# Reordering the key, query and value projections around the start of windowed attention in a two-layer decoder trunk

## The chip, the cores and the metric

The kernel runs on one core of a Trainium2 chip. The metric is device time in microseconds (us), the median over runs. The engines are TensorE (PE), VectorE (DVE), ScalarE (ACT), GpSimd (POOL) and SyncE (SP, which here issues the weight loads).

## The reference, cut to what matters

One sequence of 256 tokens of width 1024 passes through two layers. Layer 0 is a gated linear recurrence and a dense SwiGLU. Layer 1 is sliding-window attention (16 query heads, 4 key/value heads, head size 64, window 128) and a top-2-of-8 routed SwiGLU. The change touches the attention's front end alone:

```
hn = rmsnorm(h, kv_norm); k, v = split(hn @ kv_w, 2)      # 256 columns each
k = rmsnorm(k per head) ; q = rmsnorm((rmsnorm(h, attn_norm) @ w_q) per head)
logits = q @ k.T * scale + bias            # banded, window 128, 4 query heads a group
m = max(logits, sink); p = exp(logits - m)
out = (p / (sum(p) + exp(sink - m))) @ v ;  h = h + out @ w_o
```

The routed experts that follow take two thirds of the time and aren't changed.

## The kernel before

Every engine has its own program, written out by hand; they meet at semaphores. An engine runs its instructions in the order of its program, so one that waits holds up all that stands behind it.

**Dense weights.** All weights ahead of the experts form one stream of 1 MB chunks (`stream`), numbered `c`. SP loads chunk c into `raw`; ACT rounds it (`round_to`, L526, writes `w_hi`); DVE subtracts the rounded part (`rest_to`, L784, writes `w_lo`); PE multiplies in three products of the high and low parts (`product`, L1253 to L1255). `w_hi` and `w_lo` have three slots, so ACT rounds chunk c only when PE has used chunk c-3. A chunk costs PE 24 matmuls of 512 columns or 48 of 256. `to_rows` makes rows of tokens: `t` is one of two tiles of 128 tokens.

**Projections before.** Two chunks give keys and values together (256 rows of both widths are accumulated into `banks[0]` and `banks[1]`, each holding keys and values of a token tile). Then four chunks give the queries: each holds 256 rows of `w_q` at the full width of 1024, so that all 16 heads are complete only at the end of the fourth. They fill banks 2 to 5.

**The inputs of the projections.** They are the residual transposed and scaled by either gain, rounded by ACT (`fresh_round`, L553) and subtracted by DVE (`fresh_rest`, L798), first `kv_hi`/`kv_lo`, then `ht_hi`/`ht_lo`, each in four groups (token tile, half of the width).

**Normalisation.** Keys: ACT evicts `kk` and `ksq` (and the values `vt`), DVE sums the squares, ACT takes the root (`head_roots`, L538), DVE scales and writes `k2` twice. PE turns `k2` (L1472) ahead of the last query chunk and DVE copies it into `kT` (L1071). Queries: after the last chunk ACT squares (L700), DVE sums (L1078), ACT takes the roots, DVE scales into `xs` (L1086), PE turns them (L1485), DVE copies into `aqT` (`turn_copy`, L823).

**Attention.** For each of four groups g of heads, `logits(g)` on PE fills three banks: a bias product (L1458) and the logits (L1502). DVE takes maxima (`largest`, L1095 to L1102), ACT exponentials (L721 to L727), DVE normalises (`normalise`, L1107 to L1112), PE turns the probabilities in three banks (`turn_probs`, L1512), DVE copies them (`turn_copy` into `pTs`), PE multiplies by the values (`attend`, L1524 to L1526). On PE the order is logits(0), logits(1), then for each g turn_probs(g), logits(g+2), attend(g). Only two banks, `turn`, serve all transposes, in turn: a new one waits until the copy of the one before the last is done. The output projection follows in four chunks from `C_O`.

Of the kernel before, what the change touches and what calls it, by code (L numbers as in the profile page):

```python
# [8 lines left out]
P = 128  # L9
D = 1024  # L10
KT = D // P
# [9 lines left out]
FF = 2816  # L21
# [9 lines left out]
N_IN, N_OUT, N_FF, N_DOWN, N_KV, N_Q, N_O = 16, 4, 2 * FF // 256, FF // 256, 2, 4, 4  # L31
# [4 lines left out]
C_Q = C_KV + N_KV  # L36
C_O = C_Q + N_Q
# [40 lines left out]
def build_program(nc, a, out):  # L78
# [19 lines left out]
    stream += [flat(a["kv_w"], 512 * i, 512) for i in range(N_KV)]  # L98
    stream += [flat(a["swa_w_q"][0], 256 * i, 256) for i in range(N_Q)]
# [20 lines left out]
    with ctx:  # L120
# [390 lines left out]
        def _(act):  # L511
# [161 lines left out]
            round_to(C_KV + 1)  # L673
# [19 lines left out]
            round_to(C_O - 1 + LEAD)  # L693
            for t in range(TT):
                if t == 0:
                    act.wait_ge(tile_done, 1)
                else:
                    act.wait_ge(chunk_used, C_O)
                for half in range(2):
                    nc.scalar.activation(xs[:, t, 512 * half:512 * half + 512], banks[2 + 2 * t + half][:, :],  # L700
                                         ACT.Square, scale=tok_rstd[:, 2, t:t + 1]).then_inc(sq_ready, 1)
            for t in range(TT):
                head_roots(QH * t, QH, AD, 4 + 1 + t + 1)
# [9 lines left out]
            for g in range(KVH):  # L713
# [5 lines left out]
                l = banks[3 * (g % 2):3 * (g % 2) + 3]  # L719
# [7 lines left out]
                nc.scalar.activation(sinkd[:, g, :, :], sinkd[:, g, :, :], ACT.Exp).then_inc(exps_ready, 1)  # L727
            att_round(KVH - 2)
# [42 lines left out]
        def _(dve):  # L771
# [277 lines left out]
            rest_to(C_KV + 1)  # L1049
            for group in GROUPS:  # L1050
                fresh_rest(ht_hi, ht_lo, 8, LO_Q, group)
            rest_to(C_Q - 1 + LEAD)
            dve.wait_ge(kv_out, 3 * TT)
# [11 lines left out]
            rest_to(C_O - 2 + LEAD)  # L1065
# [9 lines left out]
            rest_to(C_O - 1 + LEAD)  # L1075
            for t in range(TT):
                dve.wait_ge(sq_ready, 4 + 2 * t + 2)
                nc.vector.tensor_reduce(ssq[:, QH * t:QH * t + QH], heads(xs[:, t, :]), AX.X, ADD).then_inc(ssq_ready, 1)  # L1078
            for t in range(TT):
                dve.wait_ge(root_ready, 4 + t)  # L1080
                part = rstd[:, QH * t:QH * t + QH]
                then(nc.vector.reciprocal(part, part))
                then(nc.vector.tensor_scalar(part, part, tok_rstd[:, 2, t:t + 1], None, MUL))
                for half in range(2):
                    n0 = QH * t + 8 * half
                    nc.vector.tensor_tensor(heads(xs[:, t, 512 * half:512 * half + 512]), heads(banks[2 + 2 * t + half][:, :]),  # L1086
                                            rstd[:, n0:n0 + 8].unsqueeze(2).to_broadcast([P, 8, AD]), MUL).then_inc(q_normed, 1)
            for t in range(TT):
                for u in range(2):
                    turn_copy(aqT[:, 4 * u:4 * u + 4, P * t:P * t + P])  # L1090

            def largest(g):
                l = banks[3 * (g % 2):3 * (g % 2) + 3]
# [27 lines left out]
            largest(0)  # L1121
            normalise(0)
# [14 lines left out]
            for t in range(TT):  # L1137
                for half in range(2):
                    add_part(C_MOE - 1, 6, (t, half), [banks[1], banks[2], banks[4], banks[5]][2 * t + half], None)
# [107 lines left out]
        def _(pe):  # L1247
# [69 lines left out]
            def to_rows(c, width, kts, k0, n_k, hi, lo, dst, since=None, tell=False, fresh=None, then_turn=None):  # L1317
# [4 lines left out]
                for t in range(TT):  # L1322
                    for q in range(max(1, width // 512)):
                        w = min(width, 512)
                        for k in range(kts):
# [3 lines left out]
                            if fresh is not None and q == k == 0:  # L1329
                                pe.wait_ge(fresh_lo, fresh[t])  # L1330
# [124 lines left out]
            def biases(g, b):  # L1455

                t, first, last = logit_banks[b]
                nc.tensor.matmul(banks[3 * (g % 2) + b][:, :], const[:, K_ANTI:K_ANTI + P],  # L1458
# [3 lines left out]
            for i in range(N_KV):  # L1462
                to_rows(C_KV + i, 512, 4, 4 * i, KT, kv_hi, kv_lo, lambda t, q: banks[t][:, :],
                        fresh=[LO_KV + 2 * t + i + 1 for t in range(TT)])
            for i in range(N_Q):
                if i == N_Q - 1:

                    pe.wait_ge(keys_ready, 2)
                    for t in range(TT):
                        bank = turn_bank()  # L1470
                        for g in range(KVH):
                            ins = nc.tensor.transpose(bank[:, P * g:P * g + P], k2[:, t, g, :, :].rearrange("p i e -> p (i e)"), ident)  # L1472
                        ins.then_inc(turned, 1)
# [217 lines left out]
```

## Time and profile before

| what | value |
|---|---|
| time of three runs | 1413.07, 1415.06, 1415.53 us; median 1415.06 |
| span of the profiled execution | 1414.1 us |
| PE, DVE, ACT, POOL busy | 95%, 24%, 18%, 2% of the span |
| mean granted TensorE clock | 0.983 of full speed |
| memory traffic | 442.50 MB, mean 313 GB/s |

The span runs from the first to the last instruction of one profiled execution; the time of that execution outside the profiler isn't given by itself, and the median of the runs is 1.0 us above its span. A busy share is that of the whole span. A matmul's length in the timeline overlaps with the next one's, since matmuls are pipelined: the step from start to start is what counts. "Idle before" is the time that an engine stood still ahead of an instruction, with what released it.

### The profile page before, as it was taken

To read this page: it belongs to the slowest core of one execution; us is meant where nothing else is said; L and a number is where in the kernel's file an instruction comes from. 1 tells how busy PE (TensorE), PEld (TensorE's weight loads), DVE (VectorE), ACT (ScalarE), POOL (GpSimd) and SP (SyncE) were. 2 spreads that over 40 slices of the span, in tenths; PEclk is the share of its full clock that TensorE was granted. 3 is DMA by queue.
4 is the path that set the end of the run, shared out by engine and by line. 5 is a ranking of instruction groups with operands and counts; after the bars stand their busy time and mean duration, and the time that the engine had idled before them with its cause. 6 is when DMAs were issued, how large, how long until landed. Compare 5 with 4: busy or idle time off the path is not lost.

```text
span 1414.1 us, 32772 instructions
## 1 busy us (share of the span) xinstructions
PE 1349.5 (95%) x14759; PEld 798.3 (56%) x14759; DVE 344.5 (24%) x485; ACT 260.5 (18%) x396; POOL 21.2 (2%) x27
## 2 busy tenths in 40 slices
PE   6998999999979699999999999999999999999994
PEld 6997899988757434534533543443453453453352
DVE  5864555545765401000000000000000100000001
ACT  5463544444632100000000000000000000000000
POOL 0001000000000100000000000000000000000001
PEclk9999999999989899999999999999999999999997
DMA  9962465554701896999999999999999999999994
GB/s 320 350 230 74 138 198 182 180 195 162 246 22 60 339 365 229 360 406 322 408 420 383 390 418 398 378 416 408 367 413 419 366 412 419 360 409 420 380 383 170
DMA packets 123701, 442.50 MB, mean 313 GB/s; under 512 B 9060, under 2 KB 50356, under 8 KB 107188
## 3 DMA queue, kind: packets, MB, share of 16 engines
q1 hardware_dynamic: 117600, 424.75, 79.3%
q10 hardware_dynamic: 4820, 11.53, 2.3%
q0 software_dynamic: 1152, 4.19, 0.8%
q8 instruction: 119, 1.95, 0.6%
q14 instruction: 10, 0.08, 0.0%
HBM read 434.12 MB, written 12.08 MB: 316 GB/s over the span
## 4 chain that ended last, share of the span: by engine, by line
PE 92%; DVE 4%; ACT 2%; DMA 1%; issue 1%; ACTq 0%; POOL 0%; POOLq 0%; DVEq 0%
PE bank L1607 41%; PE bank L1622 21%; PE bank L1253 8%; PE bank L1255 8%; PE bank L1254 8%; PE bank L1652 1%; PE bank L1502 1%; PE bank L1665 1%; PE bank L1597 1%; PE bank L1391 1%; PE bank L1458 1%; DVE w_lo L784 0%; PE bank L1589 0%; DMA raw<-slot_rows,slot 0%; ACT w_hi L526 0%
## 5 line engine op out<-in xcount | busy, mean ns | idle before, releaser
L1607 PE MATMUL bank<-raw,xT 128*32 128x512 f32 (+1 forms) x4608 | 440.8, 539 | 3.7 <-issue 3.0
L1607 PEld LDWEIGHTS bank<-raw,xT 128*32 128x32 f32 x4608 | 151.7, 110 | 282.1 <-issue 282.1
L1622 PE MATMUL bank<-dn,hidT 128*32 128x256 f32 x5376 | 296.5, 379 | 0.0
L1622 PEld LDWEIGHTS bank<-dn,hidT 128*32 128x32 f32 x5376 | 172.3, 110 | 116.1 <-issue 4.4
L784 DVE TENSOR_TENSOR w_lo<-raw,w_hi 128x2048 fp32r<-128x2048 f32 x62 | 141.8, 2291 | 117.7 <-ACT w_hi L526 117.6
L1228 DVE TENSOR_TENSOR e_hid<-e_silu,bank 128x512 f32<-128x512 f32 (+1 forms) x48 | 26.9, 616 | 530.4 <-PE bank L1607 530.4
L1607 PE MATMUL bank<-up_more,xT 128*32 128x384 f32 (+1 forms) x1536 | 150.3, 539 | 0.0
L1253 PE MATMUL bank<-ht_hi,w_hi 128*128 128x256 f32 x480 | 137.2, 286 | 4.2 <-DVE w_lo L857 2.7
L1255 PE MATMUL bank<-ht_hi,w_lo 128*128 128x256 f32 x480 | 136.8, 285 | 0.0
L1254 PE MATMUL bank<-ht_lo,w_hi 128*128 128x256 f32 x480 | 135.7, 283 | 0.0
L526 ACT ACTIVATE w_hi<-raw 128x2048 fp32r<-128x2048 f32 x62 | 118.1, 1912 | 61.6 <-PE bank L1255 61.6
L1607 PEld LDWEIGHTS bank<-up_more,xT 128*32 128x32 f32 x1536 | 50.9, 110 | 93.4 <-issue 93.4
L1253 PEld LDWEIGHTS bank<-ht_hi,w_hi 128*128 128x128 f32 x480 | 91.3, 190 | 5.5 <-issue 5.5
L1254 PEld LDWEIGHTS bank<-ht_lo,w_hi 128*128 128x128 f32 x480 | 92.4, 192 | 0.0
L1255 PEld LDWEIGHTS bank<-ht_hi,w_lo 128*128 128x128 f32 x480 | 90.9, 189 | 0.0
L756 ACT ACTIVATE hidT<-bank 128x512 f32<-128x512 f32 (+1 forms) x32 | 17.4, 545 | 386.2 <-PE bank L1652 205.3
L1253 PE MATMUL bank<-w_hi,ht_hi 128*128 128x256 f32 (+1 forms) x224 | 75.5, 337 | 1.2 <-DVE w_lo L784 1.2
L1254 PE MATMUL bank<-w_lo,ht_hi 128*128 128x256 f32 (+1 forms) x224 | 74.5, 332 | 0.0
L1255 PE MATMUL bank<-w_hi,ht_lo 128*128 128x256 f32 (+1 forms) x224 | 74.3, 332 | 0.0
L751 ACT ACTIVATE e_silu<-bank 128x512 f32<-128x512 f32 (+1 forms) x48 | 22.7, 544 | 244.3 <-PE bank L1607 244.3
L760 ACT ACTIVATE yb<-bank 96x512 f32<-96x512 f32 x8 | 4.7, 594 | 235.2 <-PE bank L1622 235.2
L1253 PEld LDWEIGHTS bank<-w_hi,ht_hi 128*128 128x128 f32 x224 | 42.6, 190 | 6.5 <-DVE w_lo L784 1.7
(246 smaller groups left out, 828.5 us busy)
## 6 DMA issues: line engine op xcount, KB each, us to landing
dn<-in_moe_w_down SPq DMA_DIRECT2D x112, 1024.0 KB, 12.6
raw<-in_moe_w_gate SPq DMA_DIRECT2D x48, 1024.0 KB, 13.5
raw<-in_moe_w_up SPq DMA_DIRECT2D x48, 1024.0 KB, 12.6
raw<-in_moe_w_gate SPq DMA_DIRECT2D x48, 768.0 KB, 9.3
raw<-in_moe_w_up SPq DMA_DIRECT2D x48, 768.0 KB, 6.3
up_more<-in_moe_w_gate SPq DMA_DIRECT2D x16, 1024.0 KB, 21.8
up_more<-in_moe_w_up SPq DMA_DIRECT2D x16, 1024.0 KB, 12.4
raw<-in_hgrn_w_in SPq DMA_DIRECT2D x15, 1024.0 KB, 12.1
```

What stands on the lines that cost most here:

```text
L526: nc.scalar.activation(w_hi[:, slot, :], raw[:, slot_raw, :], ACT.Copy).then_inc(hi_ready, 1)
L751: nc.scalar.activation(e_silu[:, j, 0:w], banks[j][:, 0:w], ACT.Silu).then_inc(e_silu_ready, 1)
L756: nc.scalar.activation(hidT[sup][:, :, j, :], src[:, 0:w].rearrange("p (k t) -> p k t", t=P), ACT.Copy).then_inc(hidT_ready, 1)
L784: nc.vector.tensor_tensor(w_lo[:, slot, :], raw[:, slot_raw, :], plain(w_hi[:, slot, :]), SUB).then_inc(split_ready, 1)
L1228: nc.vector.tensor_tensor(e_hid[:, j, 0:w], e_silu[:, j, 0:w], banks[GRPS + j][:, 0:w], MUL).then_inc(e_hid_ready, 1)
L1253: nc.tensor.matmul(dst, st[0], mv[0], start=first, stop=False)
L1254: nc.tensor.matmul(dst, st[0], mv[1], start=False, stop=False)
L1255: return nc.tensor.matmul(dst, st[1], mv[0], start=False, stop=last)
L1391: whole = lambda bank_rows, at, w, st, mv: nc.tensor.matmul(bank[bank_rows:bank_rows + CH, at:at + w], st, mv, start=True, stop=True)
L1458: nc.tensor.matmul(banks[3 * (g % 2) + b][:, :], const[:, K_ANTI:K_ANTI + P], bias_rev[:, GRP * g + first:GRP * g + last, 2 * P - P * (t + ...
L1607: ins = nc.tensor.matmul(out_banks[j][GTOK * c:GTOK * c + GTOK, 0:w], xT[:, kt, GTOK * g:GTOK * g + GTOK], chunk[:, w * b:w * b + w], star ...
L1622: ins = nc.tensor.matmul(banks[6 + j // 2][GTOK * c:GTOK * c + GTOK, 256 * (j % 2):256 * (j % 2) + 256], tok, dn[:, i % DN_RING, D * half ...
```

## The change

- The stream becomes: keys (one chunk, all 1024 rows of 256 columns), queries in four chunks of 512 rows and 512 columns (two for heads 0 to 7, two for heads 8 to 15), values (one chunk), then the output projection as before. The number of chunks and of bytes stays.
- PE: keys; query chunks 0, 1, 2; turn the keys; turn the first half of the queries; query chunk 3; `logits(0)`; turn the second half; the values; `logits(1)`; then the loop over g as before.
- ACT: key evictions ahead of the rounding of query chunk 2; squares and roots of each half of the queries apart (`query_roots`); values evicted after the exponentials of group 0.
- DVE: sums and scaling of the first half stand after the subtraction of query chunk 3, then the copies of the keys and of this half, then the subtractions of the value chunk and of the first output chunk, then the second half; the copies of the second half and the next subtraction stand between `largest(0)` and `normalise(0)`.
- Banks: keys in 0, values in 1, the query halves in 2, 3 and 4, 5; the logits in 2, 3, 0 and 4, 5, 1; the output in 2, 3, 0, 4.
- Query chunk 0 waits for two of the four groups of `ht_lo`, instead of all; the waits for `kv_lo` are by group too.

```diff
-    stream += [flat(a["kv_w"], 512 * i, 512) for i in range(N_KV)]
-    stream += [flat(a["swa_w_q"][0], 256 * i, 256) for i in range(N_Q)]
+    stream += [deep(a["kv_w"], 0, 256)]
+    for half in range(2):
+        stream += [flat(a["swa_w_q"][0][:, 512 * half:512 * half + 512], 512 * i, 512) for i in range(2)]
+    stream += [deep(a["kv_w"], 256, 256)]
...
+        LOGIT_BANKS = ([banks[2], banks[3], banks[0]], [banks[4], banks[5], banks[1]])
+        OUT_BANKS = [[banks[2], banks[3]], [banks[0], banks[4]]]
...
-            round_to(C_Q - 1 + LEAD)
-            act.wait_ge(chunk_used, C_Q)
+            round_to(C_Q + 1)
+            act.wait_ge(chunk_used, C_KV + 1)
             act.wait_ge(rstd_ready, 3)
             for t in range(TT):
                 mine = tok_rstd[:, 2, t:t + 1]
-                nc.scalar.activation(vt[:, t, :], banks[t][:, 256:512], ACT.Copy, scale=mine).then_inc(kv_out, 1)
-                nc.scalar.activation(kk[:, t, :], banks[t][:, 0:256], ACT.Copy, scale=mine).then_inc(kv_out, 1)
-                nc.scalar.activation(ksq[:, t, :], banks[t][:, 0:256], ACT.Square, scale=mine).then_inc(kv_out, 1)
+                keys = banks[0][:, 256 * t:256 * t + 256]
+                nc.scalar.activation(kk[:, t, :], keys, ACT.Copy, scale=mine).then_inc(kv_out, 1)
+                nc.scalar.activation(ksq[:, t, :], keys, ACT.Square, scale=mine).then_inc(kv_out, 1)
+            round_to(C_Q + 2)
             head_roots(0, TT * KVH, AD, 4 + 1)
             ta[0] += TT
...
+            def query_roots(half):
+
+                for t in range(TT):
+                    if t == 0:
+                        act.wait_ge(tile_done, half + 1)
+                    else:
+                        act.wait_ge(chunk_used, C_Q + 2 * half + 2)
+                    nc.scalar.activation(xs[:, t, 512 * half:512 * half + 512], banks[2 + 2 * half + t][:, :],
                                          ACT.Square, scale=tok_rstd[:, 2, t:t + 1]).then_inc(sq_ready, 1)
+                head_roots(QH * half, QH, AD, 4 + 1 + TT * (half + 1))
+
+            round_to(C_Q + 3)
+            query_roots(0)
+            round_to(C_O)
+            query_roots(1)
+            round_to(C_O + 1)
...
+                if g == 0:
+
+                    act.wait_ge(chunk_used, C_V + 1)
+                    for t in range(TT):
+                        nc.scalar.activation(vt[:, t, :], banks[1][:, 256 * t:256 * t + 256], ACT.Copy,
+                                             scale=tok_rstd[:, 2, t:t + 1]).then_inc(kv_out, 1)
...
-            rest_to(C_O - 2 + LEAD)
+            rest_to(C_Q + 3)
+
+            def query_sums(half):
+
+                for t in range(TT):
+                    dve.wait_ge(sq_ready, 4 + TT * half + t + 1)
+                    at = QH * half + 8 * t
+                    nc.vector.tensor_reduce(ssq[:, at:at + 8], heads(xs[:, t, 512 * half:512 * half + 512]), AX.X, ADD).then_inc(ssq_ready, 1)
+
+            def query_norms(half):
+
+                dve.wait_ge(root_ready, 4 + half)
+                both = rstd[:, QH * half:QH * half + QH]
+                then(nc.vector.reciprocal(both, both))
+                for t in range(TT):
+                    at = QH * half + 8 * t
+                    part = rstd[:, at:at + 8]
+                    then(nc.vector.tensor_scalar(part, part, tok_rstd[:, 2, t:t + 1], None, MUL))
+                    nc.vector.tensor_tensor(heads(xs[:, t, 512 * half:512 * half + 512]), heads(banks[2 + 2 * half + t][:, :]),
+                                            part.unsqueeze(2).to_broadcast([P, 8, AD]), MUL).then_inc(q_normed, 1)
+
+            query_sums(0)
+            query_norms(0)
             dve.wait_ge(keys_zeroed, 1)
             for t in range(TT):
                 dve.wait_ge(turned, td[0] + 1)
...
+                turn_copy(aqT[:, 0:4, P * t:P * t + P])
+            rest_to(C_O)
+            query_sums(1)
+            query_norms(1)
...
             largest(0)
+            for t in range(TT):
+                turn_copy(aqT[:, 4:8, P * t:P * t + P])
+            rest_to(C_O + 1)
             normalise(0)
             largest(1)
...
+            to_rows(C_KV, 256, KT, 0, KT, kv_hi, kv_lo, two_tiles(banks[0]),
+                    fresh={(t, 4 * half): LO_KV + 2 * t + half + 1 for t, half in GROUPS})
+            for i in range(N_Q - 1):
+                queries(i)
+            pe.wait_ge(keys_ready, 2)
+            for t in range(TT):
+                bank = turn_bank()
+                for g in range(KVH):
+                    ins = nc.tensor.transpose(bank[:, P * g:P * g + P], k2[:, t, g, :, :].rearrange("p i e -> p (i e)"), ident)
+                ins.then_inc(turned, 1)
+            turn_queries(0)
+            queries(N_Q - 1)
...
+            pe.wait_ge(bias_loaded, 16)
             logits(0)
+            turn_queries(1)
+            to_rows(C_V, 256, KT, 0, KT, kv_hi, kv_lo, two_tiles(banks[1]))
             logits(1)
```

`queries(i)` is `to_rows` of chunk `C_Q + i` into bank 2 + 2 half + t; `turn_queries(half)` is, for each token tile, a wait for `q_normed`, a bank of `turn` and four transposes.

## Rows read from the trace of the kernel before

**Rows 1.** The page: shares of the chain that ended last, by engine.
```profile
PE 92%; DVE 4%; ACT 2%; DMA 1%; issue 1%; ACTq 0%; POOL 0%; POOLq 0%; DVEq 0%
```

**Rows 2.** Windows: length; PE, PEld, DVE, ACT, POOL busy (count); clock; DMA share; GB/s.
```profile
387.00:412.10 25.10, 17.50 (x74) 12.48 (x73) 16.01 (x32) 7.98 (x31) 0.00 (x0) 0.81 0.13 43
412.10:436.00 23.90, 21.46 (x143) 15.36 (x141) 16.25 (x33) 9.76 (x46) 0.00 (x0) 0.92 0.00 1
...
489.30:1395.00 905.70, 901.83 (x11752) 398.69 (x11752) 52.54 (x96) 50.28 (x103) 0.00 (x0) 1.00 0.98 382
```

**Rows 3.** Timeline of PE: start us, length us, line, operation, idle before.
```profile
363.63 0.50 PE L1253 MATMUL bank<-w_hi,ht_hi 128*128 128x512 f32 x1 [1.24 <-DVE w_lo L784]
...
380.60 1.04 PE L1472 MATMUL bank<-const,pr 128*128 128x128 f32 x8
381.39 0.48 PE L1253 MATMUL bank<-w_hi,ht_hi 128*128 128x512 f32 x1
...
391.01 1.25 PE L1485 MATMUL bank<-const,xs 128*128 128x128 f32 x8 [2.05 <-DVE xs L1086]
394.05 1.94 PE L1485 MATMUL bank<-const,xs 128*128 128x128 f32 x8 [1.78 <-DVE aqT L823]
...
411.21 1.11 PE L1512 MATMUL bank<-const,pr 128*128 128x128 f32 x4 [2.41 <-DVE pT L823]
412.12 1.91 PE L1458 MATMUL bank<-bias_rev,const 128*128 128x512 f32 x2
...
419.34 0.43 PE L1524 MATMUL bank<-pT,vt 128*64 128x128 f32 x2
...
423.64 1.02 PE L1458 MATMUL bank<-bias_rev,const 128*128 128x512 f32 x2
...
428.93 0.43 PE L1524 MATMUL bank<-pT,vt 128*64 128x128 f32 x2
```

**Rows 4.** Timeline of PE in an earlier 256-column projection.
```profile
80.20 0.28 PE L1253 MATMUL bank<-w_hi,ht_hi 128*128 128x256 f32 x1
...
80.55 0.28 PE L1253 MATMUL bank<-w_hi,ht_hi 128*128 128x256 f32 x1
```

**Rows 5.** Timeline of DVE over the projections and the attention.
```profile
356.52 4.22 DVE L798 SCALAR_TENSOR_TENSOR ht_lo<-bank,cols,ht_hi 128x128 fp32r<-128x128 f32 x16
361.29 4.49 DVE L784 TENSOR_TENSOR w_lo<-raw,w_hi 128x2048 fp32r<-128x2048 f32 x2 [0.55 <-ACT w_hi L526]
...
369.06 2.28 DVE L784 TENSOR_TENSOR w_lo<-raw,w_hi 128x2048 fp32r<-128x2048 f32 x1
...
381.30 2.81 DVE L1071 COPY kT<-bank 64x512 f32<-64x512 f32 x4 [1.83 <-PE bank L1472]
...
390.27 1.29 DVE L1086 TENSOR_TENSOR xs<-bank,rstd 128x512 f32<-128x512 f32 x2
...
405.77 0.17 DVE L1107 TENSOR_TENSOR rsum<-rsum,sinkd 128x8 f32<-128x8 f32 x1 [3.50 <-ACT sinkd L727]
...
410.48 1.28 DVE L823 COPY pT<-bank 128x512 f32<-128x512 f32 x2
```

**Rows 6.** Timeline of ACT over the key and value evictions.
```profile
359.20 3.85 ACT L526 ACTIVATE w_hi<-raw 128x2048 fp32r<-128x2048 f32 x2
362.81 0.60 ACT L688 ACTIVATE vt<-bank,tok_rstd 128x256 f32<-128x256 f32 x1
...
364.59 0.65 ACT L690 ACTIVATE pr<-bank,tok_rstd 128x256 f32<-128x256 f32 x1
365.26 1.28 ACT L538 ACT_TABLE_LOAD   x1
366.56 0.30 ACT L538 ACTIVATE rstd<-ssq,eps 128x8 f32<-128x8 f32 x1
```

**Rows 7.** Windows of PE alone: length, busy (count), granted clock, DMA share, GB/s.
```profile
392.00:399.00 7.00, 5.22 (x23) 0.51 0.01 2
...
409.00:416.00 7.00, 4.79 (x15) 0.52 0.00 0
```

More of the change, by code:

```diff
@@ L35 @@
 C_KV = C_DOWN + N_DOWN
-C_Q = C_KV + N_KV
-C_O = C_Q + N_Q
+C_Q = C_KV + N_K
+C_V = C_Q + N_Q
+C_O = C_V + N_V
 C_MOE = C_O + N_O
@@ L672, in _ @@
                 fresh_round(kv_hi, 32, 8, group)
-            round_to(C_KV + 1)
+            round_to(C_Q)
             for j, group in enumerate(GROUPS):
@@ L1074, in _ @@
                 td[0] += 1
-            rest_to(C_O - 1 + LEAD)
             for t in range(TT):
[L1077 to L1090, printed above, removed]
+                turn_copy(aqT[:, 0:4, P * t:P * t + P])
+            rest_to(C_O)
+            query_sums(1)
+            query_norms(1)
             def largest(g):
-                l = banks[3 * (g % 2):3 * (g % 2) + 3]
+                l = LOGIT_BANKS[g % 2]
                 dve.wait_ge(logits_full, 3 * g + 1)
@@ L1328, in to_rows @@
                                 split_since(since, kt)
-                            if fresh is not None and q == k == 0:
-                                pe.wait_ge(fresh_lo, fresh[t])
+                            if fresh is not None and q == 0 and (t, k) in fresh:
+                                pe.wait_ge(fresh_lo, fresh[t, k])
                             tok = slice(P * t, P * t + P)
@@ L1457, in biases @@
                 t, first, last = logit_banks[b]
-                nc.tensor.matmul(banks[3 * (g % 2) + b][:, :], const[:, K_ANTI:K_ANTI + P],
+                nc.tensor.matmul(LOGIT_BANKS[g % 2][b][:, :], const[:, K_ANTI:K_ANTI + P],
                                  bias_rev[:, GRP * g + first:GRP * g + last, 2 * P - P * (t + 1):2 * P],
                                  start=True, stop=False)
-            for i in range(N_KV):
-                to_rows(C_KV + i, 512, 4, 4 * i, KT, kv_hi, kv_lo, lambda t, q: banks[t][:, :],
-                        fresh=[LO_KV + 2 * t + i + 1 for t in range(TT)])
@@ L1465, in _ @@
[L1465 to L1473, printed above, removed]
-                to_rows(C_Q + i, D, 2, 2 * i, KT, ht_hi, ht_lo, lambda t, q: banks[2 + 2 * t + q][:, :], None, "tile",
-                        fresh=[LO_Q + 4] * TT if i == 0 else None)
@@ L1476, in _, with queries @@
-            pe.wait_ge(bias_loaded, 16)
-            pe.wait_ge(kv_out, 3 * TT)
-            biases(0, 0)
-            biases(0, 1)
-            for t in range(TT):
-                for u in range(2):
-                    pe.wait_ge(q_normed, 2 * t + u + 1)
+            two_tiles = lambda bank: lambda t, q: bank[:, 256 * t:256 * t + 256]
+            def queries(i):
+                half, part = divmod(i, 2)
+                to_rows(C_Q + i, 512, 4, 4 * part, KT, ht_hi, ht_lo, lambda t, q: banks[2 + 2 * half + t][:, :], None, "tile",
+                        fresh={(t, 0): LO_Q + 2 * t + part + 1 for t in range(TT)} if half == 0 else None)
@@ L1483, in _, with turn_queries @@
+            queries_turned = []
+            def turn_queries(half):
+                for t in range(TT):
+                    pe.wait_ge(q_normed, TT * half + t + 1)
                     bank = turn_bank()
                     for k in range(4):
-                        ins = nc.tensor.transpose(bank[:, P * k:P * k + P], xs[:, t, P * (4 * u + k):P * (4 * u + k) + P], ident)
+                        ins = nc.tensor.transpose(bank[:, P * k:P * k + P], xs[:, t, P * (4 * half + k):P * (4 * half + k) + P], ident)
@@ L1494, in logits @@
                     seen = P * (t + 1)
-                    if g == 0:
-                        pe.wait_ge(turn_free, queries_turned - 2 * (TT - 1 - t))
-                    if g > 0 or b == 2:
-                        biases(g, b)
+                    if b == 2 and g < 2:
+                        pe.wait_ge(kv_out, (2 + g) * TT)
+                    biases(g, b)
+                    if g % 2 == 0:
+                        pe.wait_ge(turn_free, queries_turned[g // 2] - (TT - 1 - t))
                     for hh in range(first, last):
                         head = GRP * g + hh
-                        ins = nc.tensor.matmul(banks[3 * (g % 2) + b][:, seen * (hh - first):seen * (hh - first) + seen],
+                        ins = nc.tensor.matmul(LOGIT_BANKS[g % 2][b][:, seen * (hh - first):seen * (hh - first) + seen],
                                                aqT[:, head // 2, P * t:P * t + P], kT[:, hh % 2, g, 0:seen],
```

28 lines of the change are left out of this document (9 added, 19 removed).

## The prediction

> **What bounds the kernel now.** I read the page's chain first: PE carries 92% of what ended last, DVE 4%, ACT 2% [rows 1]. So time is won only where PE stands still or runs slowly. Then the windows. From 489.3 to 1395 us, the experts, PE is busy 901.8 of 905.7 us at full clock: nothing before it can shorten it, it can only start earlier [rows 2]. The attention's front end is different: of the 25.1 us from 387.0 PE is busy 17.5 at a clock of 0.81, and of the next 23.9 it is busy 21.5 at 0.92 [rows 2]. The timeline of PE says why. The four query chunks end at 387, then the transposes of the queries wait 2.05 us for DVE's scaling and 1.78 us for its copy, and later the last transpose of group 0's probabilities waits 2.41 us for a copy [rows 3]. After both pauses the granted clock lies at 0.51 and 0.52 for 7 us, the lower of its two levels (1.2 against 2.4 GHz), with 5.2 and 4.8 us of PE work in them [rows 7]; some 5 us go there. All of that is one serial chain: queries, norm, turn, logits, maxima, exponentials, norm, turn. PE has nothing else to do in it.
>
> **Same work on PE.** A chunk is 24 matmuls of 512 columns or 48 of 256. In the 256-column form three start every 0.35 us [rows 4], so 48 take 5.6 us. The key transposes (8) cost 0.79 us from their start to the next matmul [rows 3], and a 512-column chunk in this stage takes 5.63 us by the same pace (from 363.63, four of them and the transposes give 386.94, where the stretch of 387.0 begins). The reordered chunks cost the same sum, nothing is added or removed on PE, ACT or DVE but splits of the same passes (two sums of 512 columns for one of 1024: below 0.3 us for all). Bytes are the same, and SP loads by the same counts, six chunks ahead; rows of 1 KB in the two half-width chunks are the form that the dense weights have already.
>
> **Up to the second query chunk.** Keys take the place of the first mixed chunk. Query chunk 0 must now wait for the first group of `ht_lo`: DVE starts the 16 passes at 356.52 and needs 4.22 us [rows 5], a quarter is done at 357.6; PE, done with two chunks at 363.63 - 1.24 = 362.4 [rows 3] and so with one at 356.8, could have gone on 0.8 us earlier. But query chunk 1 needs the subtraction that DVE starts at 361.29 (two in 4.49, one till 363.6) [rows 5], and before it the same subtraction made PE wait 1.24 us up to 363.63 [rows 3]. So those 0.8 us come out of an existing pause: cost nothing. If the cover were gone, 0.8 us. Both kernels are level at 363.63.
>
> **Query chunk 2: a new wait.** ACT rounds one chunk from 359.20 (two take 3.85) to 361.1, then evicts keys only: four passes at 0.36 us a step (six start within 362.81 to 364.59 and one step more), till 362.5; then it rounds chunk 2 till 364.4, loads the root's table 1.30 us, and takes the root at 365.7 [rows 6]. DVE, which before had subtracted two chunks ahead, now has the key norm between: from root (366.56 [rows 6]) to the next subtraction (369.06 [rows 5]) were 2.50 us, so it starts at 368.2 and ends at 370.5. PE ends chunk 1 at 363.63 + 5.63 = 369.26 and waits 1.25 us. Loss 1.25. Chunk 2 ends at 376.15.
>
> A rule of the Trainium skill speaks against this: ScalarE: Activation LUTs, What ACT_TABLE_LOAD costs, puts a switch at about 2.66 us, the load and a drain. By that the root, the subtraction and chunk 2 would come 1.4 us later and the gain would be 7.3 instead of 8.7 us. This case's row has the root 1.30 us after the load's start [rows 6], so I take 1.30.
>
> **Query chunk 3: two more waits.** DVE subtracts chunk 3 till 372.7, sums the first half (two passes of about 0.65: two such take 1.29 [rows 5]), waits for the root (0.35) and scales, with two passes and small operations of 0.25 each, till 376.5, about when PE ends chunk 2. This is the part that was exposed before. PE turns the keys until 376.95. DVE starts its copy 0.70 us after the transposes start (380.60 to 381.30) [rows 3, 5], at 376.9, and needs 2.81 for four [rows 5]: the first bank is free at 378.3, the second at 379.7. PE waits 1.4, turns four (0.4 to 0.45), waits 0.95, turns four, and starts chunk 3 at 380.3. Loss 2.35 us of standing still. Queued behind these waits are chunk 3 and everything after it; DVE is the cause, and it isn't late for chunk 3 itself.
>
> **Then PE runs without a pause.** Chunk 3 to 385.9; `logits(0)`, 5.3 us at full clock as from 423.64 to 428.93 [rows 3], to 391.2; the second half's transposes 0.8, to 392.0; values to 397.6; `logits(1)` to 402.8. Beside it, DVE: copies to 381.0, two subtractions 4.49 to 385.5, sums and scaling of the second half to 389.9 (the last square follows chunk 3 at 386.6), in time for the transposes. `largest(0)` ends at 392.7, exponentials take 3.5 [rows 5] to 396.1; meanwhile DVE copies (1.28) and subtracts (2.25) to 396.2; `normalise(0)` to 398.5. That is 4 us before PE turns them. The values' eviction stands behind the exponentials on ACT and waits for 397.6; it is done at 398.4, and the third bank of `logits(1)` asks for it at 401.1. If the values came straight before that bank, their two evictions would cost 0.7 us.
> DVE ends `largest(1)` at 402.8 + 0.3 + 0.69 + 0.4 = 404.2, copies the first probabilities (0.64 [rows 5]), PE turns the last four (0.45) and begins `logits(2)` at 405.4. Before, that was 412.12 [rows 3]: 6.7 us won. It then took until 419.34 at the low clock; at full clock 5.3 us, so `attend(0)` comes at 410.7 instead of 419.34. **Sum: 8.65 us.** Of it 1.9 us are the clock in `logits(2)`; the other 6.7 are pauses and low clock ahead of it, net of the 3.6 us of new waits.
> After `attend(0)` the order is unchanged. `normalise(1)` and `largest(2)` end at about 412.8, 2.1 us after its start, and the eviction that ACT has ahead of the next exponentials ends then too, so group 2 is not late. All later stages, the experts' loads too (bound to the same counts), move with it.
>
> Bounds. New waits: between 1.25 (if the key copies were hidden) and 6 us (3.6, and as much again as the longest idle before a transpose, 2.41 [rows 3]). Clock: see below.
>
> **The rivals.**
> A, the forecast: 8.7 us less, 1406.4. The sum is made on a span of 1414.1 us; the median is 1.0 higher, and I apply the difference to the median.
> B, the clock falls in the new pauses. PE stands from 377.0 to 378.4 and from 378.85 to 379.8, with four transposes between. Before, 2.05 us, transposes, 1.78 us brought it down, a single 1.24 us did not [rows 3, 7]. This lies between. If it falls, PE runs chunk 3 at 1.2 GHz for up to the 7 us of the rows, losing half: 1.7 (half that spell) to 3.5 us. 1408.1 to 1409.9. [...]
> C, DVE is late somewhere that I have as hidden (second half's norm, `largest(1)`, group 2), and takes 2 to 5 us back: 1408.5 to 1411.5. DVE is busy 16.0 of 25.1 and 16.3 of 23.9 us [rows 2], and the new order packs this closer. For it: 1.25 and 2.35 us are already such waits. Against: margins of 2 to 4 us above.
> D, nothing arrives at the end: the experts are paced by memory, whose share is 0.98 in their stage [rows 2], so an earlier start only waits for weights: 1414 to 1416. Against it: PE stands 3.9 us in 905 [rows 2].
> E, slower: the clock stays down after the stall at 377. Low clock costs half its length, so it eats the 8.7 us once it lasts 17.4 us of PE work, and makes the kernel slower by over 2.8 us (0.2%) from 23 us on, that is from 380 all the way to `turn_probs(0)`: 1418 or more. The two spells of rows 7 lasted 7 us each, with PE dense after them; the stretch here is denser.
>
> **How the numbers follow.** Chances: A 0.47, B 0.28, C 0.17, D 0.05, E 0.03. The point is A's, 1406.4, with its own range 1404.5 to 1407.8 (later low spells, some 1.5 us, fall as they may). The range for 8 in 10 goes from 1403.8 to 1410.8, over B and most of C. A measurement tells about 0.2% (2.8 us) from no change: faster is below 1412.2, which A, B and C give: 0.92; same 0.05 (D); slower 0.03.
>
> **What would show it.** In the profile after: PE's idle 1.2 us before query chunk 2 on a `w_lo`, 1.4 and 0.9 us before the query transposes on `kT`; hardly any idle and a clock of 1.00 from 381 to 403; `logits(0)` from about 386; `logits(2)` near 405 and `attend(0)` near 410.7; the experts' stage of the same length, starting 8 to 9 us earlier. Wrong would be: another idle of over 1 us between `logits(0)` and `attend(0)`, a low clock on chunk 3, or a memory wait in the experts.

## The result, and the profile after

The kernel after takes 1403.07 us (1401.13 to 1404.98, 4 runs) against 1414.63 us (1413.07 to 1415.53, 4 runs): a ratio of 0.992, with an interval of 0.9906 to 0.9933. It is faster by 11.6 us. Forecast were 8.7 us less; 1403.07 lies 3.3 us below the point and 0.7 us below the lower end of the range; 0.4 of the 3.3 is the median of before, which a fourth run brought from 1415.06 to 1414.63. The profiled execution of after has a span of 1403.1 us, against 1414.1. Before's is a long one: 25 later executions of before had spans of 1409.5 to 1413.2 us, so differences taken between these two profiles can be larger than those of the medians.

First the windows of after, with the same columns as [rows 2]: length; PE, PEld, DVE, ACT, POOL busy (count); clock; DMA share; GB/s.

```profile
363.60:380.00 16.40, 14.03 (x64) 10.54 (x62) 13.20 (x19) 10.32 (x9) 0.00 (x0) 1.00 0.69 254
380.00:403.00 23.00, 22.21 (x125) 17.94 (x125) 18.95 (x27) 9.03 (x24) 0.00 (x0) 1.00 0.40 138
403.00:411.00 8.00, 6.94 (x36) 4.97 (x35) 5.22 (x12) 3.42 (x17) 0.00 (x0) 1.00 0.00 0
...
481.00:1384.00 903.00, 902.02 (x11764) 396.93 (x11762) 52.54 (x96) 49.65 (x102) 0.00 (x0) 1.00 0.98 384
```

Where before had PE busy for 17.5 of 25.1 us at a clock of 0.81 [rows 2], it now works 22.2 of 23.0 at 1.00. The experts' last line is the one to look at twice: PE stands about 1.0 us in that stage, where it stood 3.9 [rows 2].

The timeline of PE of after, in the columns of [rows 3]:

```profile
351.80 0.36 PE L1286 MATMUL bank<-w_hi,kv_hi 128*128 128x256 f32 x1
...
358.54 0.47 PE L1286 MATMUL bank<-w_hi,ht_hi 128*128 128x512 f32 x1 [0.74 <-DVE ht_lo L817]
...
364.37 0.50 PE L1286 MATMUL bank<-w_hi,ht_hi 128*128 128x512 f32 x1
...
371.41 0.50 PE L1286 MATMUL bank<-w_hi,ht_hi 128*128 128x512 f32 x1 [1.16 <-DVE w_lo L803]
...
379.38 0.63 PE L1511 MATMUL bank<-const,xs 128*128 128x128 f32 x4 [1.21 <-DVE kT L1112]
380.80 0.63 PE L1511 MATMUL bank<-const,xs 128*128 128x128 f32 x4 [0.79 <-DVE kT L1112]
...
386.89 1.02 PE L1491 MATMUL bank<-bias_rev,const 128*128 128x512 f32 x2
...
406.00 0.66 PE L1553 MATMUL bank<-const,pr 128*128 128x128 f32 x4 [1.06 <-DVE pT L842]
406.49 1.02 PE L1491 MATMUL bank<-bias_rev,const 128*128 128x512 f32 x2
...
411.78 0.43 PE L1565 MATMUL bank<-pT,vt 128*64 128x128 f32 x2
```

Line for line this is the forecast picture: a wait on `ht_lo` ahead of query chunk 0 (0.74 us, worked out 0.8) out of the old pause ahead of chunk 1, a wait on `w_lo` ahead of query chunk 2 (1.16 us, worked out 1.25), two on the key copies (1.21 and 0.79, worked out 1.4 and 0.95), then no idle until the last transposes of group 0's probabilities (1.06, where before had 2.41 [rows 3]). This execution came to the keys at 351.80, before's profiled one at 351.05, so distances are what compare: from the keys to `attend(0)` it was 68.29 us and is 59.98. That is 8.31 us; worked out were 8.65.

The rest isn't in the attention. These are the groups of PE's matmuls in the experts (line, engine, operation; busy us, mean ns; idle before us and what ended it), first of before, then of after:

```profile
L1607 PE MATMUL bank<-raw,xT 128*32 128x512 f32 (+1 forms) x4608 | 440.8, 539 | 3.7 <-issue 3.0 <-DVE xT L1214 0.7
```

```profile
L1650 PE MATMUL bank<-raw,xT 128*32 128x512 f32 (+1 forms) x4608 | 440.5, 539 | 0.7 <-DVE xT L1247 0.7
```

Same count, same mean, but 3.0 us of idle time with the releaser "issue" are gone: the engine waited for nothing that the profile shows. In the timeline they stand at one place, the first matmul of an item of the expert loop; the second item, before and after:

```profile
603.27 3.21 PE L1607 MATMUL bank<-raw,xT 128*32 128x512 f32 x28 [1.20 <-issue]
```

```profile
595.94 1.47 PE L1650 MATMUL bank<-raw,xT 128*32 128x512 f32 x12
```

The first item began at 489.34 before and at 483.40 after. So the first period (from the start of one item to the start of the next) was 113.93 us before and is 112.54 after; before's other six are 112.77 to 113.18 us, after's 112.52. The eighth begins at 1281.44 before and at 1271.06 after: seven periods are 792.10 and 787.66 us, 4.44 less. The whole span then adds up, in us: +0.75 (later at the keys), -8.31 (keys to `attend(0)`), +1.62 (lost between `attend(0)` and the experts), -4.44 (seven periods), -0.62 (the last item and what follows) = -11.00, as the spans differ.

### The profile page after: what moved, and what is told of

It reads as the page before. It is cut to its first block, busy times and chain, and to the rows that moved or that the text cites. A ratio compares the mean times of both kernels' runs of the same rounds, so it can differ in the third digit from the quotient of the medians.

```text
span 1403.1 us, 32871 instructions
## 1 busy us (share of the span) xinstructions
PE 1346.1 (96%) x14807; PEld 796.1 (57%) x14807; DVE 345.2 (25%) x489; ACT 260.4 (19%) x396; POOL 21.3 (2%) x27
## 4 chain that ended last, share of the span: by engine, by line
PE 92%; DVE 4%; ACT 2%; DMA 1%; issue 1%; ACTq 0%; POOL 0%; POOLq 0%; DVEq 0%
PE bank L1650 41%; PE bank L1665 21%; PE bank L1286 8%; PE bank L1288 8%; PE bank L1287 8%; PE bank L1695 1%; PE bank L1543 1%; PE bank L1491 1%; PE bank L1708 1%; PE bank L1640 1%; PE bank L1424 1%; DVE w_lo L803 0%; PE bank L1632 0%; ACT w_hi L532 0%; DMA raw<-slot_rows,slot 0%
```

## The experiments

The expert loop is one block of about 2960 instructions in PE's program, run eight times. The change makes 48 narrower matmuls of each chunk of keys or values where there were 24, and so moves the loop's first instruction from number 6113 to 6208 in that program. That gave two questions: does the place of the loop make the 4.4 us (theory P, against: an effect of earlier or smoother weight loads), and which part of the reordering makes the 8.3?

**e1: the kernel before with the loop moved, e2: the kernel after with the loop moved.** Increments of an otherwise unused semaphore stand at the head of PE's program; nothing else differs.

```diff
+            for _ in range(95):          # e1; 161 in e2
+                pe.sem_inc(pe_pace, 1)
             pe.wait_ge(ident_loaded, 16)
```

> The kernel before, with 95 semaphore increments at the head of PE's program, where PE waits 8 us for data anyway. Nothing else differs; PE's loop over the experts starts at instruction 6208 of its program, as in the changed kernel, instead of 6113. Theory place (the 4.4 us that the seven returns of the loop cost before, and not after, hang on where the loop lies in PE's code): an item takes 112.52 us each time, no issue idle at its start, span 1409.5 to 1410, ratio 0.997. Theory start (the returns are free because the stage starts earlier or its loads fall otherwise): as before, 113.1 us an item, 1414. Theory chance (it changes from run to run): items between the two.

> The changed kernel with 161 such increments at the head of PE's program, so that the loop starts at instruction 6369, the same place in a page of 256 instructions as 6113 (remainder 225). Theory place: an item takes 113.1 us instead of 112.52 on average, issue idles of 0.2 to 1.2 us at the starts, 4.4 us more than the changed kernel: 1407.5. Theory start: 112.52 us an item, 1403. If the increments themselves cost at the head of the program it shows as a later first matmul.

e1 took 1417.41 us against 1413.67, ratio 1.0026 (1.0016 to 1.0037); e2 1424.6, ratio 1.0076 (1.0059 to 1.0093). The times miss what was expected since increments aren't free. The first matmul shows it (timeline of PE, e1 then e2):

```profile
15.44 0.34 PE L1353 MATMUL bank<-const,vecs 64*128 64x64 f32 x1 [15.44 <-issue]
```

```profile
25.53 0.34 PE L1386 MATMUL bank<-const,vecs 64*128 64x64 f32 x1 [25.53 <-issue]
```

From 95 to 161 increments are 10.1 us, 0.15 each. In e1 the first matmul comes 7.4 us later than before (8.08), yet the median is 3.7 us above before's: without the late start e1 would be some 3.6 us faster. The periods answer the question all the same. In e1 they are 112.55 and then six times 112.52, without idle time: the loads and the attention of before, the periods of after. In e2 they are 112.95 to 113.23, together 3.7 us more than after's, and each item but the first has its idle time (0.21 to 0.50 us), such as

```profile
612.08 4.50 PE L1653 MATMUL bank<-raw,xT 128*32 128x512 f32 x40 [0.21 <-issue]
```

So the stall goes with the place, not with the order of the projections. Nor does it come and go by chance: e3, e4, e6, e7 and e8 below, which have the loop where after has it or within one instruction of it, all have 112.52 us.

**e5: the kernel before with narrow key and value chunks alone.** It moves the loop to 6208, as the change does, and leaves the order.

```diff
-    stream += [flat(a["kv_w"], 512 * i, 512) for i in range(N_KV)]
+    stream += [deep(a["kv_w"], 256 * i, 256) for i in range(N_KV)]
...
-                to_rows(C_KV + i, 512, 4, 4 * i, KT, kv_hi, kv_lo, lambda t, q: banks[t][:, :],
-                        fresh=[LO_KV + 2 * t + i + 1 for t in range(TT)])
+                to_rows(C_KV + i, 256, KT, 0, KT, kv_hi, kv_lo, lambda t, q: banks[i][:, 256 * t:256 * t + 256],
+                        fresh={(t, 4 * half): LO_KV + 2 * t + half + 1 for t, half in GROUPS} if i == 0 else None)
```

> The kernel before with one harmless part of the change: keys and values in a chunk each (256 columns, all 1024 rows), both still ahead of the queries, everything else in the old order. PE has 48 more matmuls of half the width, the same time, and its expert loop lands at instruction 6208 instead of 6113 without anything at the head of the program. Theory place: items take 112.52 us each, 4.4 us less in all: median about 1409.3 where the kernel before gives 1413.7, and logits and attend at the old times. Rival (the increments at the head, not the place, changed the loop in the two shifted kernels): 113.1 us an item and 1413.7.

It took 1410.08 us (1408.74 to 1413.52) against 1413.89 (1411.62 to 1414.73), ratio 0.9978 (0.9968 to 0.9987). The attention keeps its long waits (PE's timeline),

```profile
391.39 1.95 PE L1485 MATMUL bank<-const,xs 128*128 128x128 f32 x8 [2.05 <-DVE xs L1086]
394.44 1.94 PE L1485 MATMUL bank<-const,xs 128*128 128x128 f32 x8 [1.09 <-DVE aqT L823]
...
411.05 0.66 PE L1512 MATMUL bank<-const,pr 128*128 128x128 f32 x4 [2.41 <-DVE pT L823]
```

and the periods are 112.55 and 112.52 us. In the median 3.8 us of the 11.6 come with a part of the change that leaves the attention's order and its long waits. The expectation of "attend at the old times" holds only roughly: counted from the end of the recurrence (the last transposes of line L1282, 351.02 in e5, 350.64 before) `attend(0)` comes at 67.5 us instead of 68.7. The low clock falls otherwise in this execution (0.76 over 409 to 416 us, where before had 0.52 [rows 7]). e11 and e12 below, with the attention of before untouched, have 67.6 as well, e1, e9 and e10 68.7 to 68.9; so this is a spread of the old kernel and not a gain of e5.

**e3: the values ahead of the first logits, e4: only the values last.** e3 takes from the change that logits stand between the chunks. e4 keeps the queries at full width, in four chunks and normalised at once, with the values behind them; it also subtracts query chunk 2 ahead of the key norm.

```diff
 # e3
+            to_rows(C_V, 256, KT, 0, KT, kv_hi, kv_lo, two_tiles(banks[1]))
             logits(0)
             turn_queries(1)
-            to_rows(C_V, 256, KT, 0, KT, kv_hi, kv_lo, two_tiles(banks[1]))
 # e4
-            turn_queries(0)
             queries(N_Q - 1)
+            to_rows(C_V, 256, KT, 0, KT, kv_hi, kv_lo, two_tiles(banks[1]))
+            turn_queries()
```

> The changed kernel with one PE line moved: the value projection stands before the first logits instead of between the logits of groups 0 and 1. Theory cover (the value projection is what fills PE while maxima and exponentials of group 0 run): all waits behind the first logits come back in part: largest(0) ends at 398.7, exponentials 402.2, normalise 404.6, largest(1) 406.8, so logits(2) starts at about 408.5 instead of 406.5 and attend(0) 2 to 4 us later, more if the clock falls. Rival (any place before logits(1) does, because DVE is the bound by then): no change within 0.5 us.

> One part of the change alone: keys first and values last, but the queries in four full-width chunks as before, normalised all at once, and the subtraction of query chunk 2 ahead of the key norm as before. The values stand straight after the queries, over their norm. Theory halves (normalising the first half early is what brings the gain): most of the gain is gone, attend(0) at 416 or later. Theory filler (any 5.6 us of PE work over the norm's chain brings it): attend(0) at 412 to 413, within 1.5 us of the changed kernel, with an exposed wait of 1 to 2 us before the first probabilities' transposes.

e3 took 1403.84 us (1403.0 to 1406.92), ratio 0.9931 (0.9915 to 0.9948). Its timeline of PE has two waits that after doesn't:

```profile
402.58 1.12 PE L1491 MATMUL bank<-bias_rev,const 128*128 128x512 f32 x2 [1.17 <-ACT vt L745]
...
407.28 0.66 PE L1553 MATMUL bank<-const,pr 128*128 128x128 f32 x4 [1.83 <-DVE pT L842]
407.77 1.02 PE L1491 MATMUL bank<-bias_rev,const 128*128 128x512 f32 x2
```

The first is the wait for the eviction of the values. It isn't the 0.7 us of the prediction, which were for values straight before that bank: here the values are long done, but their eviction stands behind the exponentials of group 0 on ACT, and these start late. The second is 0.8 longer than after's. Counted from the end of the recurrence (the last L1315 transposes, 350.46 here, 351.39 in after), `logits(2)` comes at 57.3 instead of 55.1 us and `attend(0)` at 62.6 instead of 60.4: 2.2 us later, inside the 2 to 4 of theory cover, and the rival (within 0.5) falls. At the experts the two kernels are level (132.1 and 132.0 from the same point), and the medians don't tell them apart: after had a spell of low clock at 425 to 435 that e3 didn't. Windows of that stretch, after and e3 (columns as in [rows 2]):

```profile
425.00:435.00 10.00, 9.22 (x53) 7.41 (x52) 6.60 (x9) 4.53 (x13) 0.00 (x0) 0.83 0.00 0
```

```profile
425.00:435.00 10.00, 8.39 (x56) 6.76 (x56) 7.67 (x10) 5.80 (x20) 0.00 (x0) 1.00 0.00 0
```

e4 took 1407.59 us (1406.28 to 1407.76), ratio 0.995 (0.9933 to 0.9967). In its timeline the queries wait 0.44 us for a copy and the probabilities three times, the last time 2.41 us, as long as before:

```profile
388.25 1.22 PE L1489 MATMUL bank<-const,xs 128*128 128x128 f32 x8 [0.44 <-DVE aqT L833]
...
404.89 0.78 PE L1532 MATMUL bank<-const,pr 128*128 128x128 f32 x4 [2.41 <-DVE pT L833]
```

Its `attend(0)` comes 62.1 us from the end of the recurrence (412.34 - 350.21), against 60.4 in after and 68.7 before. So 5.6 us of independent matmuls between the queries' last chunk and their transposes, with the keys first, buy 6.6 of the 8.3 us. That is nearer to theory filler (within 1.5 us of after) than to theory halves, but 1.7 us are missing. They lie in `logits(2)`: it begins at 55.3 us, as in after (55.1), and then runs at the low clock, right behind the wait of 2.41 us (window of e4):

```profile
405.00:412.00 7.00, 7.00 (x25) 4.86 (x26) 4.62 (x8) 2.71 (x14) 0.00 (x0) 0.76 0.00 0
```

That e4 reaches the experts 132.0 us from the end of the recurrence, like after, doesn't make the two equal: each has one low spell, e4 here and after later. Its four spans are 1400.9 to 1402.4 us, no longer than after's (1399.3 to 1403.1); but its times lie 5.0 to 5.8 us above its spans, those of all other kernels 1.8 to 3.0. Where these 3 to 4 us go wasn't found; the span holds no trace of them.

**e6, e7, e8: the new waits taken away.** e6 turns the keys into banks 0 and 1, so the queries' transposes don't wait for the key copies. e7 rounds and subtracts query chunk 2 ahead of the key norm, so that chunk doesn't wait for `w_lo`. e8 does both.

```diff
 # e6 (PE; DVE reads banks[t] and signals keys_copied)
-                bank = turn_bank()
                 for g in range(KVH):
-                    ins = nc.tensor.transpose(bank[:, P * g:P * g + P], ...)
-                ins.then_inc(turned, 1)
+                    ins = nc.tensor.transpose(banks[t][:, P * g:P * g + P], ...)
+                ins.then_inc(keys_turned, 1)
...
+            pe.wait_ge(keys_copied, TT)
             logits(0)
 # e7 (ACT, then DVE)
-            round_to(C_Q + 1)
+            round_to(C_Q + 2)
             act.wait_ge(chunk_used, C_KV + 1)
...
-            rest_to(C_Q + 1)
+            rest_to(C_Q + 2)
             dve.wait_ge(kv_out, 2 * TT)
```

> The changed kernel with the keys turned into banks 0 and 1, which are free then, instead of the two shared turn banks, with a semaphore of their own; the first logits wait for the key copies. Theory shared banks (the 2.0 us before the two transposes of the queries are the wait for the key copies out of the turn banks): query chunk 3 starts 2 to 2.5 us earlier relative to the key chunk (26.9 instead of 29.4), but DVE stays busy with the subtractions, the second half's norm ends only 0.5 us earlier, so logits(2) comes 2.0 us earlier. Rival (DVE's own order is the bound from the key norm on): chunk 3 earlier, logits(2) within 0.7 us of before.

> The changed kernel with ACT rounding and DVE subtracting query chunk 2 ahead of the key norm, as the kernel before had it. Theory order (the 1.2 us wait before query chunk 2 is the subtraction queued behind the key norm, in which DVE stands 2 us for the root): no wait before chunk 2, everything from there 1.2 us earlier, logits(2) too. Rival (it only moves: the key norm ends later and the transposes wait that much more): logits(2) unchanged.

> Both of the last two edits. If the two waits are separate: query chunk 3 starts 3.6 us earlier and logits(2) 3.2 us earlier than in the changed kernel, time about 3 us less than it. If DVE is the bound behind them: less than 2 us.

| kernel | median, us (lowest to highest) | ratio to before (interval) | end of recurrence to `logits(2)` |
|---|---|---|---|
| after | 1403.07 (1401.13 to 1404.98) | 0.992 (0.9906 to 0.9933) | 55.10 |
| e6 | 1400.64 (1398.57 to 1402.98) | 0.9912 (0.9893 to 0.9932) | 52.75 |
| e7 | 1404.26 (1399.45 to 1404.51) | 0.9937 (0.992 to 0.9953) | 53.66 |
| e8 | 1399.08 (1397.39 to 1399.69) | 0.9895 (0.9879 to 0.9912) | 51.32 |

The timeline of PE in e8 has the transposes of keys and queries in one row of work and no idle ahead of query chunks 2 and 3 (the 0.75 us ahead of chunk 0 stays):

```profile
374.19 1.03 PE L1521 MATMUL bank<-const,pr 128*128 128x128 f32 x8
375.07 1.04 PE L1510 MATMUL bank<-const,xs 128*128 128x128 f32 x8
381.56 1.02 PE L1490 MATMUL bank<-bias_rev,const 128*128 128x512 f32 x2
...
400.70 0.66 PE L1551 MATMUL bank<-const,pr 128*128 128x128 f32 x4 [1.06 <-DVE pT L842]
```

Removing the 2.0 us of waits on the key copies brings `logits(2)` 2.35 us nearer, the 1.16 on `w_lo` 1.44, both together 3.78: each wait on its own is worth what stands in the trace and some 0.3 us more, and they add up. The rivals of e6 (within 0.7 us) and e7 (unchanged) fall. e8 is the fastest kernel here, 14.8 us below before's median beside it (1413.89), where after is 11.6 below its own (1414.63). e7's median says nothing: its four spans are 1397.6 and three of 1402.4 to 1402.7, and after's spread nearly as far (1399.3 to 1403.1), so such an edit is judged by its place in the timeline and not by four times.

**e9 to e12: four more places of the loop.** The kernel before, with 25, 47, 159 and 207 increments in the edit of e1, in one run each. Both theories reckon in blocks of 256 instructions; so the table gives the place modulo 256 too.

> The kernel before with 25 PE semaphore increments ahead of its first matmul, so that the expert loop's first instruction is PE's number 6138 (250 modulo 256; before 6113, 225; after 6208, 64). The periods of the expert loop are read, not the time. Theory R (what is left in the block of 256 decides: with 31 instructions left the return costs 0.2 to 1.2 us, with 192 nothing): 6 are left here, so 113.0 us or more a period, as in the kernel before. Theory L (where the loop's last instruction lies decides; it is about 2960 after the first, 144 modulo 256, so about 113 in the kernel before and 208 after): it lies at about 138, and the periods may be either. If the place has no part in it: 112.52 or 113.1 at random.

> The same with 47 increments: first instruction 6160 (16 modulo 256), last at about 160. Theory R: 240 are left, periods of 112.52 us with no idle time ahead of an item. Theory L: between the two known ends (113 stalls, 208 does not), open.

> The same with 159 increments: first instruction 6272 (128 modulo 256), last at about 16. Theory R: 128 are left; 112.52 us. Theory L, if an early last instruction is what stalls: 113.0 us and idle time of 0.2 to 0.5 us ahead of each item but the first.

> The same with 207 increments: first instruction 6320 (176 modulo 256), last at about 64. Theory R: 80 are left, between the known ends, 112.52 to 112.9 us. Theory L: 113.0 us or more.

The same run of before took 1413.56 us. Periods are those from the first to the eighth item.

| kernel | loop starts at (modulo 256) | time, us | first matmul | mean period | idle ahead of an item |
|---|---|---|---|---|---|
| e10 | 6160 (16) | 1411.03 | 8.11 | 112.52 | none |
| after, e1, e5 | 6208 (64) | | | 112.52 | none |
| e11 | 6272 (128) | 1462.11 | 25.22 | 117.47 | 2.8 to 3.0 |
| e12 | 6320 (176) | 1488.80 | 32.69 | 119.49 | 1.5 to 1.9 |
| before | 6113 (225) | 1413.56 | 8.08 | 113.16 | 0.2 to 1.2, at six of seven |
| e2 | 6369 (225) | | 25.53 | 113.05 | 0.2 to 0.5 |
| e9 | 6138 (250) | 1411.44 | 7.97 | 112.56 | none |

The bad places are far worse than the one of before: 5.0 us an item at 6272 and 7.0 at 6320, though the loop's instructions are the same. The item's start isn't the only place; PE stands again a few us on, in every second item of e11 and in every item of e12. One item each in the timeline of PE:

```profile
619.48 4.49 PE L1610 MATMUL bank<-raw,xT 128*32 128x512 f32 x37 [2.94 <-issue]
625.79 4.50 PE L1610 MATMUL bank<-raw,xT 128*32 128x512 f32 x40 [1.82 <-issue]
```

```profile
744.75 1.91 PE L1610 MATMUL bank<-raw,xT 128*32 128x512 f32 x13 [1.59 <-issue]
750.00 5.34 PE L1610 MATMUL bank<-raw,xT 128*32 128x512 f32 x24 [3.34 <-issue]
```

Theory R (what is left in a block of 256 behind the loop's first instruction) falls: 6 left cost nothing, 128 left cost 5 us. Theory L (an early last instruction in its block stalls) has the sign right at 6272 and 6320, far from its size, and so isn't shown: with one length of loop its first and last instruction move together, and no run tells them apart. e9 and e10 are also the clean form of e1: up to 47 increments are done by 8.1 us, when before's first matmul still waits for its load, so the kernel before becomes 2.1 and 2.5 us faster in one run each (spans 1409.6 and 1409.2 against 1411.7 beside them) by nothing but dummy instructions. One run each is less than before's own spread; it is the periods that carry the reading.

The traces hold one thing more that bears on the cause. The DMA queue q8, of the kind "instruction", moves packets of 16 KB. Over the seven periods before (489.34 to 1281.44) and e11 (503.81 to 1326.10) have (packets, MB, share):

```profile
q8 instruction: 83, 1.36, 0.7%
```

```profile
q8 instruction: 90, 1.47, 0.7%
```

e2, e9, e10, e1, e5 and after have 83 too, e12 has 90: one more an item at the two worst places. And the packets' times fit the stops. At each of the 27 returns with idle time (before, e2, e11, e12) the first matmul comes 1.7 to 2.0 us after the end of such a packet; at each of the 11 later stops of e11 and e12 the work goes on 1.2 to 1.6 us after one. Where nothing stalls, the last packet ended 3.9 to 4.1 us ahead of the item (after), 2.4 to 2.7 (e10) or 1.8 to 2.3 (e9, just in time). So PE most likely waits there for its own instructions. No run changed these loads alone, so it is argued from the times and not shown; and why a place makes a packet late stays open.

## Why the prediction was short by 3 us

**Same work, level at the second query chunk.** Right. From the keys' start to query chunk 1 it is 12.57 us after (364.37 - 351.80) and 12.58 before (363.63 - 351.05); the 0.74 us ahead of chunk 0 came out of the old pause of 1.24.

**Query chunk 2, new wait.** Right: 1.16 us for 1.25. e7 takes it away and gets 1.44 back. The root came 1.29 us after its table load began (365.27 to 366.56), as in [rows 6]; by the Trainium skill's 2.66 us (ScalarE: Activation LUTs, What ACT_TABLE_LOAD costs) the wait would have been 1.4 us longer, and it was not.

**Query chunk 3, two more.** Right: 1.21 and 0.79 us for 1.4 and 0.95. e6 gets 2.35 back.

**PE without a pause, the sum.** Right: clock 1.00 from 380 to 411, `logits(0)` at 386.9, `attend(0)` 8.31 us nearer to the keys for 8.65. One sign in the prediction was set too low: the 1.06 us ahead of the last transposes is "another idle of over 1 us between `logits(0)` and `attend(0)`", though the sum had that very wait in it (about 1.2 us, until DVE's copy ends at 404.2 + 0.64).

**Rival B** (the clock falls in the new pauses) didn't happen: the window from 363.6 to 380, where they begin, and the two behind it stand at 1.00. Pauses of 1.21 and 0.79 us with four transposes between left the clock up, where 2.05 and 1.78 us with eight between had brought it down [rows 3, 7]. A low spell came later, where I had said that such spells "fall as they may": from `attend(2)` into the output projection, 427 to 434, at 0.76, where before had 1.00 over the same work (434 to 441). The windows, after and then before:

```profile
427.00:434.00 7.00, 7.00 (x40) 5.83 (x39) 4.88 (x6) 2.52 (x4) 0.00 (x0) 0.76 0.00 0
```

```profile
434.00:441.00 7.00, 6.82 (x46) 5.69 (x47) 5.22 (x7) 3.09 (x7) 0.00 (x0) 1.00 0.00 0
```

From `attend(2)` to `attend(3)` it is 16.64 us after and 15.03 before: this spell is the whole 1.6 us lost between `attend(0)` and the experts. e2 and e8 have a like spell (16.63 and 16.61 us), e3 to e7 none (15.02 to 15.04); what decides over it wasn't tried.

**Rivals C, D, E** didn't happen. The probabilities' last wait shrank to 1.06 us, DVE being late nowhere else by `logits(2)`; no item waits for weights, at a DMA share of 0.98.

**The step that failed** is "the experts' stage of the same length", and under it the reading of [rows 2] that "nothing before it can shorten it, it can only start earlier". I saw PE's 3.9 us of standing still in that stage and used them only against rival D. 3.0 of them were "issue" at the return of the expert loop; the change removes them by moving the loop from 6113 to 6208 in PE's program. That is worth 4.4 us in the seven periods of these two profiles (3.0 of it listed as idle time, the other 1.4 not) and some 3.6 to 3.8 us in the medians, shown by e5 (3.8 us faster, the attention's order unchanged), by e1 and e10 (the order of before, the periods of after) and by e2 (the order of after, periods of 113). With this term the steps would have given 8.65 + 4.4 = 13.1; less the 1.6 of the late low spell 11.5, against 11.6 measured. This last agreement is partly luck: single executions of after differ by 3.8 us in span, and with e5's 3.8 for the 4.4 the same sum gives 10.9.

What stays open: why a place stalls (the late instruction packets are a likely cause, not a shown one), whether the loop's start or end decides, the 3 to 4 us outside e4's span, and what starts the spell at 427.

## What to carry to other kernels

Count the idle time "issue" at the start of a long loop's iterations as a cost of its own, and before trusting an edit of a few matmuls ahead of such a loop, see in the trace whether the periods moved: here the place of the loop was worth up to 7 us an item, more than most edits, and 25 dummy instructions in a pause that PE has anyway took the mean period from 113.16 to 112.56 us. A serial chain on other engines is best covered with whatever independent work is at hand (e4's values brought 6.6 of the 8.3 us; the halves of heads the rest, by keeping a wait short enough that no low clock followed in the profiled execution); after that the next price is in shared banks and in the order of DVE's queue, and these waits cost what the timeline says or slightly more. Compare distances from a common point in the trace where a few us are at stake and executions differ by as much.

## What the runs showed of the hardware

PE's return in a loop of about 2960 instructions costs nothing measurable when the loop starts at 6160 or 6208 and 0.04 us at 6138, about 0.5 to 0.6 us an item at 6113 and 6369, and 5.0 and 7.0 us at 6272 and 6320. The two places that are 256 apart (6113, 6369) behave nearly alike, 113.16 and 113.05 us. The Trainium skill, Runtime: NRT & Kernel Launch, Instruction fetch mechanics, says that PE's instruction memory holds 2048 instructions and is refilled in 16 KiB blocks of 256. It also says that a taken branch whose target isn't in the current 2-page window has to wait for a fetch of it. The 16 KB packets of the queue "instruction" and the likeness at a distance of 256 agree with such blocks; a stall that is there at four of the seven places and absent at three is more than the page says.

A semaphore increment in PE's program took 0.15 us (10.1 us for 66 more).

A wait of 1.21 us and one of 0.79 us with four transposes between left the granted clock at 1.00 (after). Waits of 2.05 and 1.78 us with eight between (before) and one of 2.41 us (before, e4) were followed by low clock: 0.51 over 392 to 399 and 0.52 over 409 to 416 us before, 0.76 over 405 to 412 in e4. Behind waits of 0.83 and 0.78 us the clock fell in after (0.76 over 427 to 434) and stayed up in before behind the same waits (1.00 over 434 to 441); the spell cost 1.6 us.
